# A two-block transformer program on one core: pooled means and Fourier heads placed between gate units of the second block, pool output behind the sequence products

## What is computed

```python
h = _rmsnorm(x, norm_g) * (1.0 + scale[:, None]) + shift[:, None]
parts = _split_cols(h @ w_in)
o_att = jax.nn.silu(parts[3]) * _latent_attention(q, k, v, kc, vc)
o_f = silu(z_f) * (fftn(u_f, over tokens and head width).real @ w_fourier)
o_c = silu(z_c) * (b_c * (conv3(c_c * h_c) + conv_b))
o_p = silu(z_p) * ((windowed means of u_p, less u_p) @ pool_w * pool_scale)
x = x + gate * (jnp.concatenate([o_f, o_att, o_c, o_p]) @ w_out)
```

## Time and profile before

| | |
|---|---|
| median of 3 runs | 1391.8 us (1391.75 to 1392.01) |
| the profiled execution, its own time | 1391.53 us |
| its span in the trace | 1389.7 us |
| TensorE (PE) busy | 1348.2 us, 97% |
| VectorE (DVE), ScalarE (ACT), GpSimd (POOL) busy | 868.1, 739.9, 122.1 us |
| HBM | 193 GB/s over the span |

### The profile page before, as it was taken

How to read it: one execution, slowest core, us unless ns; L and a number is a source line. 1 busy time by engine, 2 the same in 40 slices (tenths; PEclk the granted TensorE clock), 3 DMA queues, 4 the chain that set the end, 5 groups by cost and what they waited for, 6 DMA issues and landing times.

```text
span 1389.7 us, 24840 instructions
## 1 busy us (share of the span) xinstructions
PE 1348.2 (97%) x10420; PEld 1225.6 (88%) x10420; DVE 868.1 (62%) x1295; ACT 739.9 (53%) x1200; POOL 122.1 (9%) x72
## 2 busy tenths in 40 slices
PE   6999999999999999999999999999999999998998
PEld 2898998998999998998899989999997778687978
DVE  3557976667779876579665476444574536428754
ACT  3466476564745534565656646454554464326552
POOL 0000000200000000000000110000103432142000
PEclk9999999999999999999999999999999999999999
DMA  9955555677699995644743558875551212032420
GB/s 345 377 187 182 171 202 195 199 272 234 224 337 367 356 362 181 211 139 163 240 152 122 194 180 293 299 250 175 174 170 61 92 61 91 31 100 92 152 91 31
DMA packets 194722, 269.54 MB, mean 194 GB/s; under 512 B 5037, under 2 KB 174386, under 8 KB 188338
## 3 DMA queue, kind: packets, MB, share of 16 engines
q1 hardware_dynamic: 194610, 267.94, 57.0%
HBM read 266.87 MB, written 1.05 MB: 193 GB/s over the span
## 4 chain that ended last, share of the span: by engine, by line
PE 80%; DVE 10%; ACT 4%; issue 2%; DMA 1%; SPq 1%; DVEq 0%; ACTq 0%
PE first_dense L1671 14%; PE first_dense L1675 13%; PE first_dense L1673 13%; PE first_dense L1007 5%; PE first_dense L1010 5%; PE first_dense L1009 5%; DVE first_w_lo L544 2%; PE first_s L1671 2%; PE first_s L1675 2%; PE first_s L1673 2%; PE first_misc L240 2%; PE first_dense L1844 2%; ACT first_w_hi L538 1%; PE first_o L1675 1%; PE first_o L1673 1%
## 5 line engine op out<-in xcount | busy, mean ns | idle before, releaser
L544 DVE TENSOR_TENSOR first_w_lo<-first_raw,first_w_hi 128x1024 fp32r<-128x1024 f32 (+2 forms) x304 | 367.0, 1218 | 229.2 <-ACT first_w_hi L538 227.3
L538 ACT ACTIVATE first_w_hi<-first_raw 128x1024 fp32r<-128x1024 f32 (+2 forms) x304 | 313.8, 1041 | 239.3 <-PE first_dense L1675 92.9
L1671 PE MATMUL first_dense<-first_h_parts,first_w_hi 128*128 128x256 f32 x1312 | 374.6, 285 | 2.2 <-DVE first_h_parts L2299 1.7
L1673 PE MATMUL first_dense<-first_h_parts,first_w_hi 128*128 128x256 f32 x1312 | 371.2, 283 | 0.0
L1675 PE MATMUL first_dense<-first_h_parts,first_w_lo 128*128 128x256 f32 x1312 | 371.1, 283 | 0.0
L1671 PEld LDWEIGHTS first_dense<-first_h_parts,first_w_hi 128*128 128x128 f32 x1312 | 251.5, 192 | 12.4 <-issue 9.2
L1673 PEld LDWEIGHTS first_dense<-first_h_parts,first_w_hi 128*128 128x128 f32 x1312 | 251.6, 192 | 0.1
L1675 PEld LDWEIGHTS first_dense<-first_h_parts,first_w_lo 128*128 128x128 f32 x1312 | 251.6, 192 | 0.0
L1009 PE MATMUL first_dense<-first_parts,first_w_hi 128*128 128x512 f32 (+1 forms) x400 | 137.0, 343 | 0.0
L1007 PE MATMUL first_dense<-first_h_parts,first_w_hi 128*128 128x512 f32 (+1 forms) x336 | 118.1, 352 | 0.9 <-DVE first_w_lo L694 0.9
L1010 PE MATMUL first_dense<-first_h_parts,first_w_lo 128*128 128x512 f32 (+1 forms) x336 | 115.6, 344 | 0.0
(11 more groups left out here) (407 smaller groups left out, 2640.4 us busy)
## 6 DMA issues: line engine op xcount, KB each, us to landing
first_raw<-in_w_in SPq DMA_DIRECT2D x78, 1024.0 KB, 5.3
first_raw<-in_w_ff SPq DMA_DIRECT2D x64, 1024.0 KB, 6.8
first_units<-in_w_ada SPq DMA_DIRECT2D x34, 1024.0 KB, 6.2
first_units<-in_w_mod SPq DMA_DIRECT2D x17, 1024.0 KB, 6.7
first_raw<-in_w_out SPq DMA_DIRECT2D x16, 1024.0 KB, 4.9
first_mb<-in_w_ada SPq DMA_DIRECT2D x10, 1024.0 KB, 8.0
first_mb<-in_w_mod SPq DMA_DIRECT2D x7, 1024.0 KB, 7.6
first_raw<-in_w_uq SPq DMA_DIRECT2D x6, 768.0 KB, 4.5
```

What stands on the lines that cost most here:

```text
L538: act.activation(w_hi[g % SPLIT][:, c], raw[g % CHUNK_RING][:, c], ACT.Copy).then_inc(hi_made, 1)
L544: dve.tensor_tensor(w_lo[g % SPLIT][:, c], raw[g % CHUNK_RING][:, c], w_hi[g % SPLIT][:, c].bitcast(F32), ALU.subtract).then_inc(lo_made, 1)
L1671: pe.matmul(out, still[0](t), moving[0](t), start=start and t == n == 0, stop=False, skip_group_check=True)
L1673: pe.matmul(out, still[0](t), moving[1](t), start=False, stop=False, skip_group_check=True)
```

## The change

It alters the order of the list and three tables, no arithmetic. Before, from step 14 (wide) and 8 (narrow):

- wide: zp0 zp1 zf0 zf1 up0 up1 uf0 uf1, pooled means 0 and 1, heads 0 to 3, pool output 0 and 1, sequence products 0 and 1, Fourier output 0 and 1
- narrow: zp zf up uf, pooled mean, heads 0 and 1, pool output, sequence product, Fourier output

After:

- wide: up0 up1 uf0 uf1, pooled means 0 and 1, zp0 zp1, head 0, zf0, heads 1 to 3, zf1, sequence products 0 and 1, pool output 0 and 1, Fourier output 0 and 1
- narrow: up uf, pooled mean, zp, heads 0 and 1, zf, sequence product, pool output, Fourier output

The jobs of the wide layer keep their steps. In the narrow layer jobs 2 and 3 begin at steps 9 and 11, before at 10 and 12. The convolution of the wide layer stays tied to `up` and so moves from steps 18 and 19 to 14 and 15; in the narrow layer it moves from pool output (step 15) to the first head (12), and its first taps from the last head (14) to the pooled mean (10).

```diff
--- before.py
+++ after.py
@@ -860,10 +860,14 @@
 
             kv = [("k", 0), ("v", 0)]
             todo = of("q") + (kv + of("cb") + of("cc") + of("za") if ctx_out else of("za") + kv + of("cb") + of("cc"))
-            for name in ("ch", "zc", "zp", "zf", "up", "uf", "pool_mean"):
+            for name in ("ch", "zc", "up", "uf"):
                 todo += of(name)
-            todo += [("fourier_head", t) for t in range(T // P)]
-            for name in ("pool_out", "fourier_seq", "fourier_out"):
+            heads = [("fourier_head", t) for t in range(T // P)]
+            if ctx_out:
+                todo += of("pool_mean") + of("zp") + heads[0:1] + [("zf", 0)] + heads[1:4] + [("zf", 1)]
+            else:
+                todo += of("pool_mean") + of("zp") + heads + of("zf")
+            for name in ("fourier_seq", "pool_out", "fourier_out"):
                 todo += of(name)
             todo += [("out", e) for e in range(N_OUT2 * PARTS)]
             unit_no = {u: n for n, u in enumerate(todo)}
@@ -890,7 +894,7 @@
 
 
             jobs = [(s, p, i) for s in range(SEQ2) for p in range(2) for i in range(2)]
-            job_step, job_lag = ([9 + 2 * n for n in range(8)], 2) if ctx_out else ([6, 8, 10, 12], 1)
+            job_step, job_lag = ([9 + 2 * n for n in range(8)], 2) if ctx_out else ([6, 8, 9, 11], 1)
 
             def job_stages(n):
                 return [(i, s) for s in (2, 1, 0) for i, at in enumerate(job_step) if at + job_lag * s == n]
@@ -935,8 +939,8 @@
                 if name in ("pool_out", "fourier_out"):
                     result_no[name, e] = len(result_no)
 
-            conv_step = {unit_no["up" if ctx_out else "pool_out", e]: e for e in range(PARTS)}
-            conv_begin = {} if ctx_out else {unit_no["fourier_head", T // P - 1]: 0}
+            conv_step = {unit_no["up", e] if ctx_out else unit_no["fourier_head", e]: e for e in range(PARTS)}
+            conv_begin = {} if ctx_out else {unit_no["pool_mean", 0]: 0}
 
             def result_part(key):
```

## The result

| | us |
|---|---|
| before, median of the runs beside it | 1392.01 (1391.75 to 1392.18) |
| changed kernel, median of 5 runs | 1398.57 (1397.48 to 1398.74) |
| ratio | 1.0045, 95% interval 1.0031 to 1.0059 |
| profiled execution of the changed kernel | 1397.72, span 1395.9 |

The change makes the kernel 6.6 us slower. The forecast was 1395.5, at most 1397.8. The direction was right, and the time lies 0.8 us above the range.

The account below looks back on a forecast made before the run. TensorE, busy 97% of the span, was taken as the bound. Wide layer +3.2, narrow layer -1.1 and one clock fall +1.7 gave +3.8 on 1391.5, 1395.3; with the median 0.3 higher, 1395.5 us, range 1393.1 to 1397.8.

Parts of the forecast that it names:

- the price of a bank: Gate units, both layers: 4.4 us from a gate unit's last product until its PSUM bank is released.
- bank waits half as dear: Rival: (a), (b), (c) and (g) cost half, 2.7 us less, giving 1392.9 us; chance 0.10.
- faster by cover: Rival: freed ScalarE and VectorE release gate banks within the cover, no clock fall, 1386.2 us; chance 0.07.
- (a): Wide layer, ahead of zf0: wait for zp1's bank behind 2.87 us of cover, 1.5 us.
- (b): Wide layer, ahead of the third head: wait for zf0's bank, about 2.15 us of cover, 2.25 us.
- (c): Wide layer, ahead of the second sequence product: wait for zf1's bank, 0.8 us.
- (d): Wide layer, pool output to first output unit: two waits on banks that VectorE releases, 0.7 us together.
- (e): Narrow layer, ahead of job 2's values: wait for ScalarE's copies behind VectorE's splits and softmax, 0.7 us.
- (f): Narrow layer, ahead of job 3's values: ScalarE's copies stand behind zp's whole gate chain, 2.65 us.
- (g): Narrow layer, ahead of pool output: wait for zf's bank behind one sequence product, 0.9 us.
- the clock term: One fall of TensorE's clock behind one of the long waits (b) and (f), +1.7 us, bounds 0 and 3.4.
- both waits are followed by a fall: Rival: the clock falls behind both (b) and (f), +5.5 us, giving 1397.3 us; chance 0.17.

Follow-up runs that it names:

- the wide half alone: The change's new order in the wide layer only, narrow layer as in the kernel before: 1396.60 us, ratio 1.0040.
- the changed kernel again: The changed kernel run once more, unaltered, on another chip: 1394.19 to 1398.23 us, ratio 1.0036.
- the narrow half alone: The change's new order and job steps in the narrow layer only, wide layer as in the kernel before: 1392.45 us, ratio 1.0009.
- the second group: Later runs on one chip with their own runs of the kernel before (median 1391.24 us); the unaltered changed kernel had 1395.57 us there.
- the wide half of the last experiment: Kernel before with, in the wide layer only, pool output 0 ahead of the sequence products and 1 behind them: 1390.41 us, ratio 0.9996.

## Why the prediction was wrong in size and right in sign

**What bounds it, and the price of a bank: right.** 4.4 us forecast; 4.38 and 4.45 measured. The rivals that rest on a cheaper chain (bank waits half as dear, faster by cover) are refuted by these rows and by the execution of the changed kernel without falls in the wide layer, whose waits are the forecast ones.

**The waits, one by one** (us, forecast and then measured):

| wait | forecast | measured |
|---|---|---|
| (a) ahead of zf0 | 1.5 | 1.62 |
| (b) ahead of the third head | 2.25 | 2.18 |
| (c) in the sequence products | 0.8 | 0.84 |
| (d) pool output to first output unit | 0.7 | 0.75 |
| (e) job 2's values | 0.7 | 0.53 |
| (f) job 3's values | 2.65 | 2.89 |
| (g) pool output, narrow | 0.9 | 0.84 |
| wide layer, net, no fall | +3.2 | +3.56 |
| narrow layer, net | -1.1 | -1.19 |

All removed waits went as forecast; job 1's 0.6 stays, as forecast. The four added waits of the wide layer sum to 5.39 in place of 5.25. The rest of the 0.36 by which its net was forecast too small lies at least in part in this, that a wait costs more than its idle time: the sequence products take 1207.82 - 1199.81 = 8.01 us with an idle time of 0.84, and 1206.29 - 1199.31 = 6.98 without one in them (kernel with pool output moved). Against a kernel before that has no fall, the narrow layer is no gain: 131.98 against 131.61, +0.4 (forecast -1.1 + 1.7 = +0.6). The whole gain of that half was the fall which, in its profiled execution, came behind the old 1.94 us.

**The step that failed is the clock term**: "I take one fall, as both waits are just above the only one that had one: +1.7". It failed in three ways. The candidates were chosen by length, 1.94 us as the border, and that border was itself the chance of one execution: the wait of 1.90 us at the start of the narrow layer, not followed by a fall in the kernel before, stands in all 13 profiled executions, and in eight of them, that of the changed kernel among them, a fall followed it. So wait (a), 1.62 us, was counted as safe; the clock fell behind it in two of the three unfilled executions profiled in which it stands behind the same units (the changed kernel's first, the wide half alone; not the changed kernel again). The longest wait, (f), brought none in the changed kernel's two profiled executions, and one in the narrow half alone and in the kernel with zf0 moved. And though the prediction says that such a wait may or may not bring a fall, it then gives the kernel one number of falls, while that number varies from execution to execution: the profiled execution of the changed kernel had two that cost, both in the wide layer, and the five timed runs of it in the second group lie from 1394.19 to 1398.23. The size, 1.7 a fall, was near: 1.56. How near a forecast with one fall comes is in part luck: the same program was 6.6 us above the kernel before in the first result and 4.3 in the second group (1395.57 against 1391.24), beside a forecast of +3.8.

With the measured terms the sum for the first profiled execution is 3.56 - 1.19 + 3.12 = +5.5, where the -1.19 already holds the fall that the kernel before had there, and 0.70 us comes from the later start of the block, which no part of the change reaches: 6.2 between the profiled executions. The rival "both waits are followed by a fall" (1397.3) was the nearest, in number and in price, though one of its two places was wrong. The rule of the Trainium skill quoted there ("TensorE: Matmul & The Clock Gate", "A second HAM failure mode: psum-queue depth-cycling") had named short, repeated pauses on banks as enough, and the fall behind 1.62 us agrees with it; the changed kernel's execution without any fall at these waits shows that they are not always enough.

**What the range left out.** Its top, 1397.8, was two falls plus 0.5. Half a microsecond was too little beside spreads that the runs of one kernel have (3.5 us over 26 runs of the kernel before). The best runs fit the sum well: 1394.19 against 1390.03, the lowest of the kernel before on that chip, is +4.2, of which the waits are +3.9 (3.56 and the narrow layer's 0.4).

**Open.** Why the clock falls behind one wait in one execution and not in the next. And 0.85 us between the profiled execution (1397.72) and the median of five runs (1398.57). The runs near 1398.6 have no trace. Their mean clocks, 0.993 and 0.994, are not below the 0.993 of the profiled one, which speaks against a third fall; a later start of the block would do it, but isn't shown.

## What to carry to other kernels

Before a unit is moved as cover, ask how it leaves its own bank: a unit with a long evacuation chain (here 4.4 us over two engines) needs work as long as that chain ahead of the next user of its bank, and between short units it cost more here than the waits it covered. A unit that leaves by one copy brought no wait on its own bank in the places tried here, but its copy still stands ahead of others on ScalarE (0.82 us, ahead of job 3's values). When a unit is taken away from a place, look for the copy that it had been covering there. Where the clock gate is involved, compare stage stretches between executions with the same number of falls, give the number of falls a range in the forecast, and count every wait on TensorE of the lengths seen here as a candidate, not only those longer than the one that had a fall.

## What the runs showed of the hardware

- The clock fell behind a wait in one execution and not behind the same wait in another. Over the 13 profiled executions:

| wait on TensorE | executions that have it | followed by a fall |
|---|---|---|
| 1.18 or 1.19 us, job 7's transposes, old order | 6 | 0 |
| 1.42 us, second head, zf0 moved | 1 | 0 |
| 1.62 us, (a) | 3 | 2 |
| 1.90 us, start of the narrow layer | 13 | 8 |
| 1.94 or 1.95 us, job 3's transposes, old order | 4 | 2 |
| 2.18 us, (b) | 3 | 1 |
| 2.89 us, (f) | 4 | 2 |

Length from 1.62 us on does not decide it. And no border can be read from the table: in the wide half of the last experiment the clock fell at 1268.0 us, 2.3 us behind a wait of only 0.87 us (the 1.90 had ended 12 us before), where four other executions had a wait of 0.87 or 0.88 us there and no fall. Its windows around that point:

```profile
1256.00:1267.00 11.00, 9.92 (x76) 9.35 (x76) 10.86 (x22) 5.80 (x15) 6.21 (x6) 1.00 0.08 25
1267.00:1272.00 5.00, 4.96 (x24) 4.43 (x23) 5.00 (x11) 4.74 (x7) 0.23 (x1) 0.66 0.00 0
```

- What a fall costs depends on what stands behind it. Each takes 1.7 us of full-speed time. Where TensorE bounds the stage, 1.4 to 1.6 us came through: 133.17 and 132.98 against 131.61, 133.55 against 131.98, 222.56 against 220.94. In the execution just named it was 0.4 (132.01 against 131.61), as a wait of 0.88 us for VectorE behind it was gone. And it was nothing at the start of the narrow layer: the changed kernel ran at a mean of 0.66 over 5 us there (windows above), and yet from its first product behind the wait of 1.90 us to its first job's scores it took 1303.72 - 1264.31 = 39.41 us, in the kernel before, without a fall, 1296.34 - 1256.93 = 39.41. Before, TensorE had then waited 0.87 us for VectorE (1266.43); that wait was gone.
- A few spare products in an otherwise idle wait kept the clock at 1.00 there in the three profiled executions that had them, at no cost to the work behind them (221.00 against 220.94 us, 217.39 against 217.38).
- The second block starts between 1034.7 and 1036.5 us in the kernels profiled, and once at 1039.8, though no instruction ahead of it was moved. Such an offset is as large as the effects studied here, and only the stage stretches are free of it.
